# First modulation of a two-block transformer kernel: from two halves to four quarters of its columns, summed on strips of TensorE

## What is computed

```python
cond = jax.nn.silu(c)                                   # c: (1, 1024)
mod = (cond @ ada_w[i] + ada_b[i])[:, None, :]          # ada_w[i]: (1024, 6144)
sh1, sc1, g1, sh2, sc2, g2 = jnp.split(mod, 6, axis=-1)
h = rmsnorm(x, norm1_g[i]) * (1.0 + sc1) + sh1          # then h @ w_qkv, ...
```

## Time and profile before

| | us |
|---|---|
| median of 3 runs | 2363.35 (2363.16 to 2364.23) |
| profiled execution, its own time | 2363.94 |
| its span in the trace | 2362.1 |
| TensorE busy in the span | 2293.2 (97%) |
| first step of the first projection begins | 30.58 |
| mean granted TensorE clock | 0.992 of full |

### The profile page before, as it was taken

One profiled execution on the slowest core, in us unless ns is written; L12 is line 12 of the kernel. 1 busy time (PEld: TensorE's weight loads), 2 busy tenths in 40 slices (PEclk: granted clock), 3 DMA queues, 4 the chain that ended last, 5 costly groups with the idle time before them and its releaser, 6 DMA issues.

```text
span 2362.1 us, 27319 instructions
## 1 busy us (share of the span) xinstructions
PE 2293.2 (97%) x11144; PEld 1826.2 (77%) x11144; DVE 1177.6 (50%) x1623; ACT 870.5 (37%) x1411; POOL 156.6 (7%) x145
## 2 busy tenths in 40 slices
PE   7998999999999999999999999999999999999998
PEld 3766788888777677888887877866778887888886
DVE  4765655553455654333335455556744345553453
ACT  3563322132344533222323236355363223332331
POOL 2111000000100010000010002022020001000001
PEclk9999999999999999999999999999999999999999
DMA  8322555532221112222222222211223222233222
GB/s 326 117 81 100 188 211 198 211 117 99 81 72 63 54 63 87 101 98 98 90 99 80 98 90 99 98 63 63 72 90 107 98 81 98 89 99 107 92 88 80
DMA packets 73421, 250.67 MB, mean 106 GB/s; under 512 B 8272, under 2 KB 8528, under 8 KB 73296
## 3 DMA queue, kind: packets, MB, share of 16 engines
q1 hardware_dynamic: 73296, 248.93, 30.5%
HBM read 244.70 MB, written 4.19 MB: 105 GB/s over the span
## 4 chain that ended last, share of the span: by engine, by line
PE 80%; ACT 4%; DVE 3%; issue 1%; POOL 1%; POOLq 0%; DVEq 0%; ACTq 0%
PE pb L749 24%; PE pb L753 24%; PE pb L751 24%; PE pb L979 1%; PE pb L1004 1%; PE pb L989 1%; ACT slab L1383 1%; DVE slab L1714 1%; PE pb L773 1%; PE pb L769 1%; PE pb L771 1%; ACT spare L1383 1%; PE pb L1054 1%; PE pb L794 0%; ACT whi L1128 0%
## 5 line engine op out<-in xcount | busy, mean ns | idle before, releaser
L1420 DVE TENSOR_TENSOR wlo<-raw,whi 128x1024 fp32r<-128x1024 f32 x361 | 449.6, 1249 | 699.3 <-ACT whi L1128 699.1
L749 PE MATMUL pb<-hhi,whi 128*128 128x512 f32 x1976 | 785.3, 397 | 2.4 <-ACT hhi L1158 1.3
L751 PE MATMUL pb<-hhi,wlo 128*128 128x512 f32 x1976 | 770.6, 390 | 1.7 <-DVE wlo L1420 1.7
L753 PE MATMUL pb<-hlo,whi 128*128 128x512 f32 x1976 | 771.1, 390 | 0.4 <-DVE hlo L1416 0.4
L1128 ACT ACTIVATE whi<-raw 128x1024 fp32r<-128x1024 f32 x361 | 379.4, 1056 | 713.5 <-PE pb L753 691.7
L749 PEld LDWEIGHTS pb<-hhi,whi 128*128 128x128 f32 x1976 | 371.0, 188 | 97.7 <-issue 23.6
L753 PEld LDWEIGHTS pb<-hlo,whi 128*128 128x128 f32 x1976 | 370.6, 188 | 81.2 <-DVE hlo L1416 1.6
L751 PEld LDWEIGHTS pb<-hhi,wlo 128*128 128x128 f32 x1976 | 371.1, 188 | 79.2 <-DVE wlo L1420 2.7
L749 PE MATMUL pb<-ahi,whi 128*128 128x512 f32 x848 | 335.5, 396 | 5.5 <-ACT ahi L1312 4.8
L753 PE MATMUL pb<-alo,whi 128*128 128x512 f32 x848 | 331.1, 390 | 0.0
L751 PE MATMUL pb<-ahi,wlo 128*128 128x512 f32 x848 | 330.5, 390 | 0.0
(11 more groups left out here) (232 smaller groups left out, 1688.1 us busy)
## 6 DMA issues: line engine op xcount, KB each, us to landing
raw<-stream SPq DMA_DIRECT2D x361, 512.0 KB, 3.2
slab<-ada_w SPq DMA_DIRECT2D x80, 512.0 KB, 4.7
early<-ada_w SPq DMA_DIRECT2D x32, 256.0 KB, 8.8
X<-xT SPq DMA_DIRECT2D x8, 256.0 KB, 5.2
ya<-slab SPq DMA_DIRECT2D x8, 256.0 KB, 2.3
slab<-ya SPq DMA_DIRECT2D x8, 256.0 KB, 4.8
outT<-X SPq DMA_DIRECT2D x8, 256.0 KB, 2.1
cst<-consts SPq DMA_DIRECT2D x1, 576.0 KB, 8.5
```

Of the source, the lines that this page charges most:

```text
L749: e.matmul(out, wh, hi, start=s.k == 0, stop=False)
L751: e.matmul(out, wl, hi, start=False, stop=False)
L753: i = e.matmul(out, wh, lo, start=False, stop=s.last)
L1420: e.tensor_tensor(wlo[:, u % NW, :], raw[:, u % NRAW, :], whi[:, u % NW, :].bitcast(F), ALU.subtract).then_inc(*v_cut.up(u))
```

## The change

The first modulation is done in four quarters of 256 columns each. A load now brings, for one k and one quarter, 256 columns of the scale matrix and 256 of the shift matrix into one 128 x 512 tile (rows of 1 KB, two per partition; still 32 loads of 256 KB). The eight loads of quarter 0 are issued by ScalarE, before anything else on that engine; SP issues the rest, with six units of the weight stream among them.

`pre` of a quarter is eight matmuls of 512 moving columns. The stationary operand is 32 columns wide (`cond[:, k]` and 31 zeros), and k mod 4 chooses the strip of 32 PSUM partitions: k and k + 4 share a strip, so four sums stand in one bank. ScalarE copies the whole bank (`rows`), and TensorE adds the strips and turns them with four matmuls (`premod`). VectorE has no products of the first modulation any more. Half 1's `pre` steps in the projection are replaced by quarters 1 to 3, each as a block of eight, and two tiles of `h` are formed after each quarter. The squares of norm 0 have eight buffers and are summed by TensorE one by one (`sq`, in place of VectorE's adds and `total`). Eight `fma` instead of six are woven into the next eleven steps. The attention's first advance comes 2.6 steps earlier.

```diff
@@ score()
+    def quarter_rows(q, ks=range(KD)):
+        for k in ks:
+            tick("pre", q, k)
+        if 7 in ks:
+            tick("rows", q)
+    def quarter_norm(q):
+        tick("premod", q)
+        for k in (2 * q, 2 * q + 1):
+            tick("norm", 0, k)
...
-    for k in range(4):
-        tick("pre", 0, k)
-    rstd(0)
-    for k in range(4, KD):
...
+    tick("scaled", 0)
+    tick("pow", 0)
+    s.cut(0)
+    quarter_rows(0, range(6))
+    tick("spread", 0)
+    quarter_rows(0, range(6, 8))
+    quarter_norm(0)
+    s.cut(1)
+    s.cut(2)
     tick("sines")
...
-    for k in range(4):
-        tick("pre", 1, 2 * k)
-        tick("pre", 1, 2 * k + 1)
-        run(some(first, 6))
-    tick("premod", 1)
-    for k in range(4, KD):
-        tick("norm", 0, k)
+    for q, n in ((1, 6), (2, 7), (3, 7)):
+        run(some(first, n))
+        quarter_rows(q)
+        run(some(first, 1))
+        quarter_norm(q)
+    run(some(first, 2))
     tick("tables")
-    run(woven(some(first, 12), some_mods(6), 2))
+    run(woven(some(first, 11), some_mods(8), 1.4))
...
-    run(woven(rest(), side, PAIR, rest=False))
+    run(woven(rest(), side, PAIR, 1 - PAIR, rest=False))
@@ program(), tensor()
-        def pre(half, k):
...
-            for j in (0,) if half else (1, 0):
-                r = 64 * (1 - j)
-                i = e.matmul(b[r:r + 1, :], cond[:, k:k + 1], early_part(half, k, j), start=k == 0, stop=k == 7, skip_group_check=True)
+        def pre(q, k):
...
+            g = slice(32 * (k % 4), 32 * (k % 4) + 32)
+            i = e.matmul(b[g, :], condp[:, 32 * k:32 * k + 32], early_part(q, k), start=k < 4, stop=k >= 4, skip_group_check=True)
...
+        def premod(q):
+            b = bank(("pre", q))
+            w.wait_ge(d_in, "vec")
+            w.wait_ge(a_att, ("rows", q))
+            for d in (2, 3, 0, 1):
+                i = e.matmul(b[:, d:d + 1], modrow[q % 2][:, quarter(d)], C("one"), start=True, stop=True, skip_group_check=True)
...
+        def sq(sid, d, last):
...
+            w.wait_ge(a_sq, (0, d))
+            for c in range(4):
+                i = e.matmul(b[:, c:c + 1], SQ0[d][:, quarter(c)], C("one"), start=d == 0 and c == 0, stop=last, skip_group_check=True)
@@ program(), scalar()
+        def rows(q):
+            w.wait_ge(t_mod, ("pre", q))
...
+            e.activation(modrow[q % 2], bank(("pre", q)), ACT.Copy).then_inc(*a_att.up(("rows", q)))
...
+        for k in range(KD):
+            e.dma_start(early_part(0, k).rearrange("p (j c) -> p j c", j=2), early_source(0, k)).then_inc(*d_early[0, k].up("in"))
         w.wait_ge(d_in, "vec")
-        e.activation(cond, W("c", 0, 8), ACT.Silu).then_inc(*a_att.up("cond"))
+        e.activation(cond, W("c", 0, 8), ACT.Silu)
+        w.wait_ge(v_att, "zeros")
+        e.activation(condp.rearrange("p (k m) -> p k m", m=32)[:, 0:8, 0:1], W("c", 0, 8).unsqueeze(2), ACT.Silu).then_inc(*a_att.up("cond"))
@@ program(), sync()
-        for half in range(2):
+        for q in range(4):
             for k in range(KD):
-                if (half, k) == (0, 6):
+                if (q, k) in ((0, 4), (1, 0), (1, 2), (2, 0), (3, 0), (3, 4)):
                     load()
...
+                if q:
+                    e.dma_start(early_part(q, k).rearrange("p (j c) -> p j c", j=2), early_source(q, k)).then_inc(*d_early[q, k].up("in"))
```

More of the change, by code:

```diff
@@ L549, in program @@
     d_ada = [signal(f"d_ada{i}", 16) for i in range(NADA)]
-    d_early = {(half, k): signal(f"d_early{half}{k}", 16) for half in range(2) for k in range(KD)}
+    d_early = {(q, k): signal(f"d_early{q}{k}", 16) for q in range(4) for k in range(KD)}
     d_late = signal("d_late", 16)
@@ L807, in turn_row @@
[L807 to L815, removed]
-            w.wait_ge(d_in, "vec")
[L817 to L822, removed]
-                return
[L824 to L830, removed]
+            w.wait_ge(d_early[q, k], "in")
@@ new lines, in sq @@
+        def sq(sid, d, last):
+            if sid:
+                return
+            b = take(("stat", 0)) if d == 0 else bank(("stat", 0))
+            w.wait_ge(d_in, "vec")
+            w.wait_ge(a_sq, (0, d))
+            for c in range(4):
+                i = e.matmul(b[:, c:c + 1], SQ0[d][:, quarter(c)], C("one"), start=d == 0 and c == 0, stop=last, skip_group_check=True)
+            if last:
+                i.then_inc(*t_norm.up(("total", 0)))
+                give(("stat", 0), v_norm, ("scaled", 0))
@@ L835, in total @@
             n = 3 if isinstance(sid, tuple) else 7
[L836 to L839, removed]
+            w.wait_ge(p_sum, (sid, n - 1))
             for c in range(4):
[L841 to L844, removed]
+                i = e.matmul(b[:, c:c + 1], acc[:, quarter(c)], C("one"), start=c == 0, stop=False, skip_group_check=True)
+            w.wait_ge(a_sq, (sid, n))
+            for c in range(4):
                 i = e.matmul(b[:, c:c + 1], sq_of(sid, n)[:, quarter(c)], C("one"), start=False, stop=True, skip_group_check=True)
@@ L1153, in norm @@
             if n == 0:
-                w.wait_ge(v_mod, ("half", k // 4))
+                w.wait_ge(v_mod, ("quarter", k // 2))
             if shift is None:
@@ L1169, in gnorm @@
             e.activation(operand(key)[0], TN[j % 2], ACT.Copy).then_inc(*a_half.up(key))
[L1171 to L1175, removed]
+        def rows(q):
+            w.wait_ge(t_mod, ("pre", q))
+            if q >= 2:
+                w.wait_ge(t_mod, ("premod", q - 2))
+            e.activation(modrow[q % 2], bank(("pre", q)), ACT.Copy).then_inc(*a_att.up(("rows", q)))
         def sines():
@@ L1440, in fma, with premod @@
                 e.scalar_tensor_tensor(o, a, cond[:, k:k + 1], o, ALU.mult, ALU.add).then_inc(*v_mod.up(("fma", n)))
[L1442 to L1470, removed]
+        def premod(q):
+            n, b = slice(2 * q, 2 * q + 2), bank(("pre", q))
+            w.wait_ge(t_mod, ("premod", q))
+            e.tensor_tensor(mod[0, 1][:, n], b[:, 2:4], W("ada_b", 8 + 2 * q, 2), ALU.add).then_inc(*v_mod.up(("scale", q)))
+            e.tensor_tensor(mod[0, 0][:, n], b[:, 0:2], W("ada_b", 2 * q, 2), ALU.add).then_inc(*v_mod.up(("quarter", q)))
+            w.wait_ge(v_mod, ("scale", q))
+            e.scalar_tensor_tensor(gs[0, 1][:, n], mod[0, 1][:, n], 1.0, W("norm1", 2 * q, 2), ALU.add, ALU.mult).then_inc(
+                *v_mod.up(("gain", q)))
         def modsum(j):
@@ L1493, in norm @@
             if n == 0:
[L1494 removed]
+                w.wait_ge(v_mod, ("gain", k // 2))
             elif k == 0 and shift is not None:
@@ L1804, in vector @@
         w.wait_ge(d_in, "vec")
-        do = {"cut": cut, "sq": sq, "shift": shift, "fma": fma, "modsum": modsum, "pre": pre, "premod": premod, "scaled": scaled, "norm": norm, "gnorm": gnorm, "final": final,
+        do = {"cut": cut, "fma": fma, "modsum": modsum, "premod": premod, "scaled": scaled, "norm": norm, "gnorm": gnorm, "final": final,
               "evac": evac, "kstat": lambda: head_stats("k"), "krope": lambda: rope("k"), "kspread": kspread, "query": query, "scores": scores,
```

67 lines of the change are left out of this document (24 added, 43 removed).

## The result

The kernel after took 2366.17 us, the median of 21 runs (2359.86 to 2370.24); the kernel before, run beside it on the same chip, 2363.61 (21 runs, 2360.46 to 2365.16). The ratio is 1.0012, 95% interval 1.0006 to 1.0017: 2.6 us slower, 16 us from the forecast and outside its range. The profiled execution took 2366.17 us (span 2364.4, mean granted clock 0.990), the one of before 2363.94 (0.992).

What follows compares the result with a forecast made beforehand. TensorE, with 80% of the chain, was taken as the bound. Start 6.1, first step to k statistics 5.9 and attention 1.4 sum to 13.4 us off 2363.94: about 2350 us, range 2344 to 2357.

Steps and rivals of the forecast that it cites:

- TensorE's sums are 1.05 us a tile: Start: pace of the eight tiles' sums of squares, ending at 16.3 us; first step at 24.5, 6.1 us sooner.
- The 3.9 behind that: Start: 3.9 us from the end of quarter 0's sums to the first step, as before with half 0.
- the start stays late: Rival, start: X and quarter 0 take turns, squares head TensorE's queue; first step 27.2 to 29, total 2353 to 2355; chance 0.13.
- I take 0, at most 1.5: Ahead of the k statistics: time lost to VectorE's eight `fma` in place of six, in us.
- TensorE reaching the place as late as before relative to it: At the k statistics: reason why one or two us more of VectorE's work would cost 0, at most 1.5.
- some 10.4 us after the 25th step begins: Ahead of the k statistics: when VectorE's eight `fma` would end.
- Middle: First step to the k statistics: 36.3 us instead of 42.2, 5.9 less, mainly the pause after 24 steps going.
- Strips: A quarter's eight sums on four strips side by side: 1.9 us; bounds 1.7 to 6.9.
- the low clock of the first steps: First steps, after the short waits before them: 1.0 us lost, as before.
- 356 was estimated for rows of 1 KB: Modulation loads: about 356 GB/s, 1.9 us more on 8.4 MB; quarter 3 landed at 43.1, 3.3 us early.
- but X isn't there sooner anyway: Start: ScalarE's eight load issues, 3.8 us before it can square, would cost nothing; X taken at 14.5 us.
- 1.4 was the two steps: Attention: earlier advance puts two steps inside the 4.2 us wait for output 6, saving 1.4 us; bounds 0 and 3.

Runs made afterwards that it cites:

- e6: Kernel after plus useless wide matmuls: four ahead of the sums of squares, one of 256 columns after tiles 1, 3 and 5; 2364.03 us, ratio 0.9996.
- e3: Kernel after with quarter 0's loads issued by SP behind X, none by ScalarE; 2360.45 us, ratio 0.9979.
- e2: Kernel after with six products of the second modulation instead of eight ahead of the k statistics; 2357.04 us, ratio 0.9973.
- e5: Kernel after with squares added by VectorE again, quarter 0's loads on SP behind X, and six products; 2352.63 us, ratio 0.9955.
- e8: Kernel after without the attention's earlier first advance; 2365.74 us, ratio 1.0007.
- e11: Kernel after with six products instead of eight and without the attention's earlier first advance; 2362.15 us, ratio 0.9992.
- e7: e5 plus useless wide matmuls, eight ahead of norm 0's sum and two behind `premod` 0; 2350.68 us, ratio 0.9949.
- e9: e7 with norm 0's power ahead of the rope angles on GpSimd; 2349.57 us, ratio 0.9945.
- e4: Kernel before with only the attention's first advance 2.6 steps earlier; 2358.20 us, ratio 0.9981.

## Why the prediction was wrong

*Start: "TensorE's sums are 1.05 us a tile": the step that failed first, 8.8 us.* The 1.05 of the earlier trace rows is a price behind half 0's wide sums. The kernel before had sixteen of those instructions first:

```profile
12.84 6.24 PE L804 MATMUL pb<-early,small 128*1 128x512 f32 x16 [12.84 <-DMA early<-ada_w]
```

At the pace of the first row, 1.88 us for eight, they would take 3.8 us; the 6.24 show that much of them ran at the low level, and the 1.05 comes right after. The change removed what came first and put the sums in its place, at a price the trace of before did not hold: 1.72 a tile (shown by e6: 0.95 and 1.70 at the two clocks). From there, sums' end 23.06 for 16.3 (6.8 us), then 3.5 us up to `spread` for 1.9, the time of six sums of quarter 0 at the low pace (3.63; scaling and GpSimd's power beside them took 2.3 for 1.3 and were done before), `spread` 1.86 for 1.16: from 16.3 forecast and 20.4 at the end of quarter 0's sums to 23.06 and 29.39 measured, 9.0 late. The 3.9 behind that held (29.39 to 33.30). X was 1.5 us later than I took it, and that did not matter to the end of the sums, though it did to their beginning (in e3 they began 2.26 us sooner). The rival "the start stays late" had the right sentence, TensorE's own queue is the path now, and too small a number: its 27.2 to 29 has no term for sums at the low level.

*VectorE: "I take 0, at most 1.5": the second step that failed, 3.6 us at the place.* The cover named, "TensorE reaching the place as late as before relative to it", was none. In before the last product ended at 76.5, 3.8 us after TensorE was ready: the earlier trace rows show VectorE, not TensorE, setting that time. So a TensorE that comes sooner only waits longer there, which those rows showed and I passed over. The end of the products was mis-timed too: "some 10.4 us after the 25th step begins" is eight products and nothing else. That step began at 61.28, the first product at 65.42, behind two `hlo` and a `wlo`, and another `wlo` of 1.22 us stands among the eight: they ended 15.5 us behind the step. The copy of the k statistics stands 3.68 us behind their start in before (76.44 - 72.76), 6.20 in after (76.75 - 70.55) and 3.45 in e2: two products, at 1.36 each (5.44 for four), are the 2.5 to 2.7 by which the wait grew (0.24 to 2.76), and the low clock behind it is the rest. The earlier start neither causes nor cures this: in e3, 5.1 us ahead at the k statistics, 4.1 were lost again up to the end of the low clock, as in the kernel after, and 0.2 at most in e2 and e5, with six products. By e2, e8 and e11 together the products also cost most of what the advance brings: 5.1 us with six, 0 (medians) to 2.6 (traces) with eight. Why the lateness shortens the wait for `ahi` was not followed step by step; that stays open.

*Middle: right, 4.9 for 5.9.* Strips 1.92 for 1.9, pause gone, no load late. The microsecond missing is the low clock of the first steps, 32 to 38 us: put at 1.0, it cost 2.0, for the same stretch took 35.2 us in e7 and e9, whose first steps ran at the high level, against 37.25. It is not the late start that brings it: in e5, with the first step at 26.03, the first steps are slow as well and the stretch took 37.8.

*Loads: right in the middle, not at the start.* With the DMA engines full, the kernel after moved 339 GB/s in 20 to 25 us, almost all of it in packets of under 2 KB, and e3 363 in 15 to 30 us with some packets of 4 KB among them; 356 was estimated for rows of 1 KB. At the start, ScalarE's eight issues (4.72 us, for 3.8) were costed at nothing, "but X isn't there sooner anyway"; with them there, the start cost 1.2 to 2.9 us more than with all loads on SP (e3): ScalarE's first square began at 8.50 and 7.83 (after, e2) instead of 6.25 (e3). In the kernel after ScalarE was ready at 7.08 and waited 1.43 us more for X, so the issuing made it at most 0.8 us late and the two queues' sharing of the DMA engines the rest. How they share, which the rival "the start stays late" left open, this trace shows: in 10 to 15 us SP's queue moved 659 packets (1.27 MB) and ScalarE's 657 (0.63 MB), as many packets of one as of the other, whatever their size (in the 5 us before, 531 and 713). X came late by it, not early.

*Attention: the size was off.* 1.4 was the two steps; what goes is the whole wait and the low clock after it, about 5 alone (e4) and with six products (e11), 0 (medians) to 2.6 (traces) inside the kernel after.

*After 240 us: 3.5 us, and no place in the change explains them.* e8 shows how much such a difference between two traces means: its trace was 2.6 behind that of after up to 850 us and 0.4 ahead of it at the end. Which of the later low stretches occur differs from one execution to the next, and the time goes with them: of after's 21 runs that with mean clock 0.994 took 2359.86, those at 0.990 took 2365.7 to 2367.7, that at 0.987 2370.24. That the mean over its runs is lower than before's (0.9901 against 0.991 to 0.992 in the three batches), and that e2 has 0.993, is measured; its cause stays open.

## What to carry to other kernels

A duration read from a trace belongs to what ran before it: when a change removes the wide matmuls ahead of narrow ones, cost the narrow ones at both levels of the clock. And before an earlier arrival is counted as won, find the next meeting of engines behind it and ask which of them is late there: two products of 1.4 us on an engine that was taken to be "beside waits" cost 4 us at the place, and with six of them instead of eight the medians fell by 9.1. Where several edits are made at once, run each alone: here the kernel was 2.6 us slower with a line in it worth 5 on the kernel before, and undoing the three costly parts made it 11 us faster than before.

## What was not expected

- Sums of one-column fp32 matmuls keep TensorE busy and did not hold its clock: 100% busy at 0.50 from 12 to 16 us (e6).
- The profile's clock column reads 1.00 ahead of the first change that it records. In the kernel after it does so while a tile takes 1.72 us, which by e6 is the low level:

```profile
10.00:15.00 5.00, 5.00 (x25) 5.00 (x25) 0.00 (x0) 2.77 (x6) 3.84 (x14) 1.00 1.07 381
```

- Four column strips give 3.7 times one strip (7.05 to 1.92 us), more than two for two.
- A second queue makes the first one's loads come later: with ScalarE's eight beside them, X's took 8.5 us from issue to landing in the page's list of DMA issues (5.2 before), at no higher total rate (381 GB/s in 10 to 15 us, 396 before):

```profile
X<-xT SPq DMA_DIRECT2D x8, 256.0 KB, 8.5
```
